# Two stacked transformer blocks in one kernel: the first block's mixers in another order, and the second block's attention scores with two query heads of each key head a round

## The reference, cut to what matters

```python
# first block, mixing part of a layer: four mixers of 256 features each, from z = hn @ w_in
o_a = differential_attention(qa, ka, va, lam)     # 4 heads, two score maps each, 32 wide: softmax(q1 k1) - lam softmax(q2 k2)
o_b = silu(layer_norm(causal_depthwise_conv31(a * sigmoid(g)) + b))
o_c = u * (W_s layer_norm(v) + b)                 # u, v = split(gelu(z)); W_s mixes tokens inside chunks of 128
o_d = forgetting_attention(qd, kd, vd, log_f)     # 4 heads of 64, a cumulative gate added to the scores
h = h + g2 * (concat(o_a, o_b, o_c, o_d) @ w_out)

# second block, attention of a layer: 8 query heads on 2 key heads (4 query heads each), 64 wide, window 128
s = q @ k.T / 8 - slope[head] * dist;  p = softmax([s, sink[head]])[:-1];  out = p @ v
```

## Time and profile before

| what | us |
|---|---|
| median of three runs | 2265.62 |
| the profiled execution, its time | 2267.9 |
| its span, first to last instruction | 2265.8 |
| PE busy | 2200.1 |
| DVE busy | 1588.0 |
| ACT busy | 1096.0 |
| PE waiting for the transfers of the convolution's input, twice | 8.3 |
| mean granted clock of TensorE, of full speed | 0.995 |

### The profile page before, as it was taken

How to read it: one execution, slowest core, us unless ns; L and a number is a source line. 1 busy time by engine, 2 the same in 40 slices (tenths; PEclk the granted TensorE clock), 3 DMA queues, 4 the chain that set the end, 5 groups by cost and what they waited for, 6 DMA issues and landing times.

```text
span 2265.8 us, 31974 instructions
## 1 busy us (share of the span) xinstructions
PE 2200.1 (97%) x11869; PEld 1851.0 (82%) x11883; DVE 1588.0 (70%) x1896; ACT 1096.0 (48%) x1288; POOL 52.4 (2%) x94
## 2 busy tenths in 40 slices
PE   7999999999999998999999999999999999999998
PEld 6887887887787886888788799978878879998887
DVE  6787897886777697665655778765575567867555
ACT  3444565444444465443444465554454446465443
POOL 1000010000000010000000000000000000000000
PEclk9999999999999999999999999999999999999999
DMA  8996566995687555666555564455556555435553
GB/s 287 341 324 206 159 198 205 335 318 172 240 289 239 156 187 183 221 218 211 174 184 189 164 168 128 147 188 185 187 166 206 190 179 158 141 115 172 196 189 108
DMA packets 325042, 454.56 MB, mean 201 GB/s; under 512 B 32722, under 2 KB 270040, under 8 KB 324952
## 3 DMA queue, kind: packets, MB, share of 16 engines
q1 hardware_dynamic: 320952, 440.98, 59.3%
q0 software_dynamic: 3728, 11.31, 1.7%
q10 hardware_dynamic: 272, 1.05, 0.1%
HBM read 449.91 MB, written 1.05 MB: 199 GB/s over the span
## 4 chain that ended last, share of the span: by engine, by line
PE 83%; DVE 9%; ACT 3%; issue 2%; DMA 1%; POOL 1%; SPq 0%; DVEq 0%; ACTq 0%; POOLq 0%
PE ps L622 20%; PE ps L624 20%; PE ps L623 20%; PE ps L615 4%; PE ps L616 4%; PE ps L617 4%; DVE wlo L1959 2%; PE ps L793 2%; PE ps L775 1%; PE ps L778 1%; PE ps L776 1%; DMA arena<-in_ada_w_dram 1%; PE ps L712 1%; ACT whi L1335 1%; PE ps L1040 1%
## 5 line engine op out<-in xcount | busy, mean ns | idle before, releaser
L1959 DVE TENSOR_TENSOR wlo<-raw,whi 128x2048 fp32r<-128x2048 f32 x348 | 791.6, 2278 | 357.0 <-ACT whi L1335 355.9
L1335 ACT ACTIVATE whi<-raw 128x2048 fp32r<-128x2048 f32 x346 | 659.8, 1911 | 274.3 <-PE ps L624 238.7
L622 PE MATMUL ps<-whi,xl 128*128 128x512 f32 x1472 | 591.5, 402 | 0.0
L624 PE MATMUL ps<-whi,xh 128*128 128x512 f32 x1472 | 574.2, 390 | 0.0
L623 PE MATMUL ps<-wlo,xh 128*128 128x512 f32 x1472 | 573.9, 390 | 0.0
L622 PEld LDWEIGHTS ps<-whi,xl 128*128 128x128 f32 x1472 | 276.5, 188 | 61.2 <-issue 3.8
L624 PEld LDWEIGHTS ps<-whi,xh 128*128 128x128 f32 x1472 | 276.4, 188 | 59.8
L623 PEld LDWEIGHTS ps<-wlo,xh 128*128 128x128 f32 x1472 | 276.9, 188 | 58.4 <-issue 4.3
L615 PE MATMUL ps<-xl,whi 128*128 128x256 f32 x864 | 250.1, 289 | 4.8 <-DVE wlo L1959 4.8
L622 PE MATMUL ps<-whi,hidl 128*128 128x512 f32 x640 | 252.1, 394 | 1.5 <-DVE hidl L2151 1.5
L624 PE MATMUL ps<-whi,hidh 128*128 128x512 f32 x640 | 249.2, 389 | 0.0
(11 more groups left out here) (403 smaller groups left out, 2343.9 us busy)
## 6 DMA issues: line engine op xcount, KB each, us to landing
raw<-in_ffn_w_in_dram SPq DMA_DIRECT2D x176, 512.0 KB
arena<-in_ada_w_dram SPq DMA_DIRECT2D x144, 512.0 KB, 6.2
raw<-in_w_in_dram SPq DMA_DIRECT2D x54, 1024.0 KB
raw<-in_ffn_w_out_dram SPq DMA_DIRECT2D x44, 1024.0 KB
raw<-in_w_ffn_gate_dram SPq DMA_DIRECT2D x88, 512.0 KB
raw<-in_w_ffn_up_dram SPq DMA_DIRECT2D x88, 512.0 KB
raw<-in_w_ffn_down_dram SPq DMA_DIRECT2D x44, 1024.0 KB
raw<-in_w_out_dram SPq DMA_DIRECT2D x16, 1024.0 KB
```

What stands on the lines that cost most here:

```text
L622: pe.matmul(o, al, wh, start=start, stop=False, **kw)
L624: return pe.matmul(o, ah, wh, start=False, stop=stop, **kw)
L1335: act.activation(whi[:, k % 3, :], raw[:, k % 3, :], ACT.Copy).then_inc(hi_done, 1)
L1959: tt(a[0], a[1], a[2].bitcast(F32), ALU.subtract).then_inc(lo_done, 1)
```

## The change

In `mix0`, on PE, the order of the units and of the small matmuls changes: unit 6 and the gated mix come ahead of the first differential scores, unit 10 ahead of the turn (it stood behind the gates' scores), and the second attention's values and the modulation sums move among the projections, with the last sum behind the last projection. ACT, DVE and SP follow with orders of their own: the convolution's input is made ahead of the joined probabilities and the second norm, the cumulative gates are summed ahead of the first logits, and the tiles are loaded and used at other places. In DVE's end of `mix0` both `summed` stand behind all three last splits.

The differential scores get a function of their own, `diff_pair`, which pairs a block of one query block with a block of the other and does not use bank 5. It waits once for its own third block. The gates' scores (`gate_pair`) keep their order. In `mix1`, `crossed_scores` takes heads 2r and 2r+1 of either key head in round r, alternating between rows 0 to 63 and 64 to 127, also with one wait for its own block; slopes, sinks, values and the chunks of the branch projection follow. Sinks are now handled in two instructions where there was one, twice a round.

```diff
-TILES_BEHIND = {2: (0,), 4: (1,), 5: (2,), 7: (3,), 8: (4, 5), 9: (6, 7), 10: (8,), 11: (9,), 12: (10, 11),
-                13: (12, 13, 14, 15)}
+TILES_BEHIND = {2: (0,), 3: (1,), 5: (2,), 6: (3,), 7: (4,), 9: (5,), 10: (6, 7), 11: (8, 9), 12: (10, 11),
+                13: (12, 13), 14: (14, 15)}
...
+            def crossed_scores(L, r):
+                def block(h, qb):
+                    g, c = h // 2, 2 * r + h % 2
+                    rows = slice(64 * g, 64 * g + 64)
+                    return pe.matmul((sc0, sc1)[qb][:, h, :], AQ[rows, c, qb * P:qb * P + P], AK[rows, 0:P * (qb + 1)],
+                                     start=True, stop=True)
+                block(0, 0)
+                block(2, 1)
+                block(1, 0).then_inc(s["narrow"], 1)
+                block(3, 1)
+                block(0, 1)
+                pe.wait_ge(s["narrow"], 2 * L.l + r + 1)
+                block(2, 0)
+                block(1, 1)
+                block(3, 0).then_inc(s["scores"], 1)
+            def diff_pair(L, q, k, c):
+                def block(h, qb):
+                    rows = slice(64 * (h % 2) + 32 * c, 64 * (h % 2) + 32 * c + 32)
+                    return pe.matmul(paired(h, qb, False), q[rows, h // 2, qb * P:qb * P + P],
+                                     k[rows, h // 2, 0:P * (qb + 1)], start=True, stop=True)
+                block(0, 0)
+                block(1, 1)
+                block(2, 0).then_inc(s["pairs"], 1)
+                block(3, 1)
+                block(0, 1)
+                pe.wait_ge(s["pairs"], 2 * L.l + c + 1)
+                block(1, 0)
+                block(2, 1)
+                block(3, 0).then_inc(s["scores"], 1)
...
 # PE, mix0
                 z(5)
+                z(6)
+                gated_mix()
                 diff_scores(0)
-                z(6)
+                z(7)
                 diff_scores(1)
-                z(7)
                 z(8)
+                z(9)
                 head_stat(L, 1, 1, blk64, sq8, [ps[:, 6, :], ps[:, 7, :]])
-                z(9)
+                z(10)
                 turn(L, 0, S0)
-                gated_mix()
                 pe.wait_ge(s["foxqk"], l + 1)
                 attend(0, "dv", 7)
...
-                paired_scores(fq, fk, 0, 64, True)
+                gate_pair(halves("fq"), halves("fk"))
                 head_stat(L, 2, 2, blk64, u8[:, 1536:2048], [ps[:, 6, :]])
-                z(10)
                 convolve()
...
                 project(1, 0)
+                attend(1, "fv", PVB)
                 project(1, 1).then_inc(unit_used, 1)
-                modulation(m, 0)
-                attend(1, "fv", PVB)
-                modulation(m, 1)
                 pe.wait_ge(s["o"], seq(L, OUTS, 3))
                 project(2, 0)
-                modulation(m, 2)
+                modulation(m, 0)
                 project(2, 1).then_inc(unit_used, 1)
-                modulation(m, 3)
+                modulation(m, 1)
                 pe.wait_ge(s["o"], seq(L, OUTS, 4))
                 project(3, 0)
+                modulation(m, 2)
                 project(3, 1).then_inc(unit_used, 1)
+                modulation(m, 3)
...
 # DVE, mix0, from unit 8 to unit 11
                 unit(8)
-                tiles(4, 6)
+                unit(9)
+                mixed_gate()
+                tiles(5, 6)
                 first_probs()
                 logits(L, st, 1, S1, amask, 32 ** -0.5)
-                unit(9)
                 tiles(6, 7)
-                gate_sums()
+                unit(10)
+                conv_input()
+                tiles(7, 8)
                 joined_probs()
                 head_norm(1, shift, foxg, ("fq", "fk"), "foxqk")
-                tiles(7, 8)
-                mixed_gate()
-                conv_input()
-                tiles(8, 9)
-                unit(10)
+                tiles(8, 10)
                 unit(11)
                 logits(L, st, 2, S1, amask, 1.0)
-                tiles(9, 10)
+                tiles(10, 11)
                 diff_out()
-                tiles(10, 11)
+                gelu_in(2, zt["gu"], gu_tmp)
                 gate_probs()
...
 # DVE, end of mix0
-                tiles(15, 16)
+                unit(13)
                 rest_out(L, 3, 2, 4, zt["ca"])
-                unit(13)
+                tiles(14, 16)
+                rest_out(L, 4, 6, 8, ps[:, PVB, :])
                 unit(14)
+                unit(15)
                 summed(m, 2)
-                rest_out(L, 4, 6, 8, ps[:, PVB, :])
-                unit(15)
                 summed(m, 3)
```

More of the change, by code:

```diff
@@ L243, in program @@
         mix_names = ("convsig", "conv_in", "conv_done", "foxqk_sq", "foxqk_r", "foxqk", "diffqk_sq", "diffqk",
-                     "fx", "fl", "foxcum", "scores", "scores_read", "nmax", "probs", "pnorm", "pturned", "pt",
+                     "fx", "fl", "foxcum", "narrow", "pairs", "scores", "scores_read", "nmax", "probs", "pnorm", "pturned", "pt",
                      "pv", "outh", "o", "gu_sq", "gu_t", "gu_e", "gu", "lnv", "lny", "gv", "gmix", "dout_sq",
@@ L936, in paired_scores, with gate_pair @@
+            def gate_pair(q, k):
                 for qb in (1, 0):
+                    tok, keys = slice(qb * P, qb * P + P), P * (qb + 1)
                     for c in range(2):
[L938 to L944, removed]
+                        for g in range(2):
+                            rows = slice(64 * g, 64 * g + 64)
+                            pe.matmul(paired(2 * c + g, qb, True), q[rows, c, tok], k[rows, c, 0:keys], start=True, stop=False)
+                        for g in range(2):
+                            rows = slice(64 * g, 64 * g + GATEROWS)
+                            ins = pe.matmul(paired(2 * c + g, qb, True), cum_left[rows, tok], cum_right[rows, 2 * c + g, 0:keys],
+                                            start=False, stop=True)
@@ L1052, in att_scores @@
                         pe.wait_ge(z_copied[1], l * NZ[1] + 9)
-                    scores(L, AQ, AK, 64 * g, 64)
+                    crossed_scores(L, g)
                 def att_values(g):
-                    values(L, g, lambda h, b: AV[:, b, 64 * g:64 * g + 64], PTA,
+                    values(L, g, lambda h, b: AV[:, b, 64 * (h // 2):64 * (h // 2) + 64], PTA,
                            lambda h: ps[64 * (h % 2):64 * (h % 2) + 64, 5 - g, (h // 2) * S:(h // 2) * S + S])
@@ L1756, in mix0 @@
                 unit(9)
+                softmax(L, 0, S0)
                 copy(7)
+                unit(10)
+                sigmoids()
+                copy(8, ACT.Sigmoid)
+                logs_and_exps()
                 softmax(L, 1, S1)
                 rs(st, L.event(1), shift, stat2)
-                sigmoids()
+                copy(9)
+                copy(10)
                 turned_out(L, 0, PT1)
-                copy(8, ACT.Sigmoid)
-                copy(9)
-                logs_and_exps()
-                unit(10)
+                unit(11)
+                copied(L, zi["gu"])
+                act.activation(gu_tmp, zt["gu"], ACT.Square, scale=GELU_A ** 0.5).then_inc(s["gu_sq"], 1)
                 act.wait_ge(s["pv"], seq(L, TURNS, 1))
@@ L1802, in mix0 @@
                 unit(14)
+                summed(m, 0)
+                summed(m, 1)
                 unit(15)
@@ L2259, in logits @@
                 for h in range(4):
-                    ins = stt(tile[:, h, :], dist[:, :], -(2.0 ** -(4 * g + h + 1)), tile[:, h, :], ALU.mult, ALU.add)
+                    head = 4 * (h // 2) + 2 * g + h % 2
+                    ins = stt(tile[:, h, :], dist[:, :], -(2.0 ** -(head + 1)), tile[:, h, :], ALU.mult, ALU.add)
                 st(ins)
```

105 lines of the change are left out of this document (52 added, 53 removed).

## The result

The changed kernel takes **2253.35 us** (median of 5 runs, 2252.95 to 2256.38) against 2265.36 us of the kernel before on the same chip (5 runs, 2263.57 to 2267.47). The ratio is 0.9948, with a 95% interval of 0.9938 to 0.9959: 12.0 us less by the medians. On another chip the changed kernel had a ratio of 0.995 (0.9937 to 0.9964).

The account below looks back on a forecast made before the run. TensorE was taken as the bound (83% of the chain), mainly its waits for the first block's convolution. Terms +0.15 − 5.9 + 2.4 − 3.5 = −6.9 us gave 2258.7 us, range 2254 to 2265.

Parts of the forecast that it names:

- layer 0: First block: convolution starts 4.05 us sooner, but all comes back as a later handover; net about 0 (+0.15 us).
- layer 1: First block's second layer: same schedule, plus 6.1 us saved on a longer transfer wait and half-clock convolution; net −5.9 us.
- low clock at the handovers: Between first-block mixers and next transposes: 4.6 us idle drops the clock to 0.50, 1.2 us a layer, +2.4 us.
- second block's rounds: Four crossed score rounds fall from 2.88 to 1.85 us, 0.95 each, less 0.3 for extra DVE instructions: −3.5 us.
- I take 1.85: Time in us for a differential round pairing 128-wide with 256-wide matmuls, each pair costing its wider member; bounds 1.5 and 2.8.
- the 0.3 for the sinks: Second block: two more small DVE instructions a round lie on the path in a layer's first round, +0.15 us each layer.
- Rival 1: The clock stays up at the handovers: −9.3 us, 2256.3 us; chance 0.2.
- forecast waits of 1.5 us: First block: PE waits about 1.5 us for ACT before the values and about 1.5 for DVE before the convolution.
- 2 us or more: First block: the convolution's input transfers land at 315.5 to 319.8, hidden by this much before its start at 322.4.
- on time that the convolution waited anyway: First block: half clock after the old waits for the scores' keys and unit 6 cost nothing, falling within the convolution's wait.
- Rival 2: Crossed rounds overlap little, or layer 1's transfers still land last: about −2.5 us, 2263 us; chance 0.22.
- Rival 3: Clock falls at the turn and stays down through values, gate scores and statistic, both layers: +15 us, 2274 us; chance 0.08.

## Why the forecast was right in kind and 5 us short

| term of the sum | forecast | two traces |
|---|---|---|
| layer 0 | +0.15 | −0.78 |
| layer 1 | −5.9 | −6.83 |
| low clock at the handovers | +2.4 | +0.48 |
| second block's rounds | −3.5 | −4.95 |
| sum | −6.9 | −12.1 |

**The step that failed first is "I take 1.85" for a round.** Every round takes 1.58: 0.27 us less in eight rounds, 2.2 in all. The four of the first block are 1.08 of the 1.86 us by which its two terms are short. Those of the second block saved 1.30 each where 0.95 were put down (a slip besides: 2.88 less 1.85 is 1.03), 1.4 of its 1.45 us; the 0.3 for the sinks was about right, since the level product waits 0.12 us longer in either layer. "A mixed pair should cost its wider member" takes a pair for a barrier, and it is none. In the changed kernel two narrow matmuls on one row group run beside one wide one on the other, three wide lengths in all, like equal pairs. The forecast had this value in its other branch: "if the two row groups ran freely, a round would stay near 1.58". It went by the rule of the Trainium skill (TensorE: Matmul & The Clock Gate, Part 3, The mechanism), that matmuls start and end in program order. Two things were wrong with that. Walked through with this order, even that rule gives three wide lengths, so 1.85 did not follow from it. And the trace with the wide ones first disagrees with it on the starts, 0.33 us for the fourth block and 0.54 for the third before it; on the ends it agrees, as far as one wait can show. The bounds, 1.5 to 2.8, did hold the value.

**The clock term was mis-sized: 2.4 us forecast, 0.48 measured.** The place and the level were right: 4.71 and 4.70 us of idle time and a clock of 0.50 in both layers. What it costs is less than the slow work, since 1.13 us of waiting stood behind the transposes in the kernel before and was filled by it. In the six traces with the 4.7 us wait the stretch up to the next mixing part lost, against the kernel before, 0 to 1.1 us behind layer 0 and 0 to 1.0 behind layer 1, 0.6 and 0.2 on average. The loss goes by how long the low clock lasts. In five of these twelve handovers it lasted some 7 us, and they lost 0.57 to 1.13 us; in the other seven it lasted half that, and they lost nothing. The forecast looked for no wait that could hide the cost. Rival 1 had the right end, almost no loss, by the wrong mechanism: the clock did fall.

**Layer 0 and the convolution.** It started 4.82 us sooner (forecast 4.05): 0.54 from the two rounds, and 0.23 of small terms. Then 4.04 came back at the handover, where 4.20 were forecast, by the mechanism forecast: last sum, gain row, residual; the run with the early sums bears it out. The forecast waits of 1.5 us before the values and before the convolution are there, at 1.63 and 1.41. The transfers had about 3.9 us of slack, where "2 us or more" was said. One reason of the forecast does not hold throughout: the half clock behind the old wait for the keys did not always fall "on time that the convolution waited anyway", for in two of the six layers traced it put off the transfers' issue by 1.1 us as well.

**Layer 1** won for the reason given, no late landing and no half-clock convolution, but that layer 1 was the long one was a chance of the one trace; in two others layer 0 was long as well or instead. That this term came out near its measured value is therefore partly luck. Over the six layers traced of the old first block the mean is 121.5 us against 117.2, so 4.4 a layer, 8.8 for both; the one trace gave 7.6. With the rounds (−5.0) and the clock (+0.5 to +0.8) this makes −13, where the times say −12.0 and −11.3; the difference is within the noise of the times.

**The rivals.** Rival 2's premises are refuted by the rows (no wait for transfers, rounds not above 1.85). Rival 3's point of decision was the clock behind the turn: the convolution's quarters at 1.93 us are at full clock. Rival 2's sum has a slip besides: −6.9 with 2.5 and 2.6 given back is −1.8 and not −2.5. The low end of the range, 2254, is rival 1 and free pairs together, −9.3 and 2 us more (2254.3), so both large errors lay inside it. What it left no room for is small: the 0.8 us of small terms and the slip of 0.3, against the 0.5 that the clock did cost.

## What to carry to other kernels

Walk the instructions of two row groups through their program order before pricing them: here rounds with two short and two long ones on each group took 1.58 us, as long as equal pairs. Place a wait for one's own matmul where no row group runs out of work before it returns: asking for the fourth block in place of the third cost 0.32 us in a round of eight, and the wait between two halves of unequal load 0.75. When work is pulled forward, look at once at what the last reader waits for: here the sum placed last gave back 4 us a layer, and moving it and one projection returned most of that. Where a low clock is forecast, look for a wait behind it that hides the cost. When a wait depends on when transfers land, take several traces: this one varied between 1.9 and 6.4 us, and a fix is worth the mean, not the value of the one profile.

## What the runs showed of the hardware that was not expected

- On two row groups a matmul began before the one ahead of it in the program: 0.33 and 0.54 us into the round, in all eight rounds with the wide ones first. A wait for it returned only behind the end of the other.
- A wait for the fourth block (wide, issued two ahead of the wait), instead of the third (narrow, three ahead), cost 0.32 us in a round of 1.58.
- The granted clock does not always fall behind the same idle time. Before the second block's first units TensorE waits 1.59 to 1.62 us in every trace. In 10 of the 26 such places (two in each of 13 traces) the clock is at 0.50 behind it, in the others it stays full. In the changed kernel's first trace it stays full in the first of the two; in its second and in the one with more zero products (same code there) it falls, and that attention layer was 1.2 and 2.6 us longer. Windows some 3.5 us behind the start of these transposes, in the first trace and in the one with more zero products:

```profile
1294.00:1296.00 2.00, 2.00 (x19) 2.00 (x18) 0.68 (x1) 0.00 (x0) 0.00 (x0) 1.00 0.98 320
```

```profile
1290.00:1292.00 2.00, 2.00 (x12) 2.00 (x11) 0.98 (x1) 0.05 (x1) 0.00 (x0) 0.50 0.99 289
```

What decides it stays open.
